# Two weight sums per gate/up quad from a DRAM scratch, and a fourth quad per chunk, in a one-core decoder layer

## Chip, cores, metric

The kernel runs on one core of a Trainium2 chip. The metric is the device time of one execution in microseconds. The kernel before took 1198.18 us, the median of three runs (1197.95 to 1198.29).

## What is computed

One decoder layer on 256 tokens of width 2048: a head stage (eight attention heads and a gated short convolution) with its output projection, a cross-attention over 256 memory tokens, and a SwiGLU feed-forward of width 5632, each behind an RMS norm, then a last norm. All in float32. The change is in the feed-forward:

```python
def swiglu(h, w_gate, w_up, w_down):
    return (jax.nn.silu(h @ w_gate) * (h @ w_up)) @ w_down

h = rms_norm(x, g_ffn[l])
x = x + swiglu(h, w_gate[l], w_up[l], w_down[l])
```

## The kernel before

**Tiles and steps.** The weights lie in DRAM as one stream (`w_stream`) of tiles of 128 x 1024 floats, 512 KB each: two blocks of 128 rows (k) by 512 columns. SP loads them in order into the four slots of `raw`. Each tile passes three stations. ACT casts it to `whi` (`chunk_cast`, its line L1145; L893 ahead of the feed-forward). DVE subtracts and leaves the rest in `wlo` (the split, L1624; L1270 earlier). PE multiplies: a product of one token tile (128 tokens) with one block is three matmuls of 512 columns, hi x hi, hi x lo and lo x hi (L489 to L491, in quads L732 to L734). A direct step uses a whole tile for both token tiles, which makes 12 matmuls. `whi` and `wlo` have four slots too.

**What orders the work.** Each engine has a hand-written order, and semaphores count the steps: `w_loaded` (landed), `hi_ready` (cast), `lo_ready` (split done), `step_used` (PE done). The cast of step v waits until PE has used step v - 4 (`step_used` at v - RING + 1). SP loads into a slot of `raw` when the split of what lay there is done. Instructions of an engine go in order, so a waiting one holds those behind it.

**Chunks and quads.** Gate and up (each 2048 x 5632) are computed in 11 chunks of 512 columns (`NFC`). In a chunk, eight pairs of k blocks (2 x 128 rows) meet two token tiles and two matrices. A pair takes either two direct steps (24 matmuls), or a quad: Winograd's form of Strassen's product with 7 products in place of 8 (21 matmuls). A quad needs sums of the activations (`s_forms`, made once, ahead of chunk 0: forms `sfh`, `sfl` and a part of `ahi`, `alo`) and sums of the weights b11, b12, b21, b22, made anew in every quad. It stands in the order of steps as four parts. Before, three of the eight pairs are quads, at steps 3, 9 and 14 of a chunk of 22 steps (`QUADS`, `QUAD_AT`, `CHUNK`), and DVE makes the weight sums beside its splits: two of 512 columns in `raw` (L1619, L1627) and one of 1024 columns in `wsum` (L1631).

**Around the quads.** At step 2 of a chunk PE transposes the last chunk's result in two units (L521; ACT and DVE split it at step 3, DVE's line L1279). After the last quad DVE combines the products (`combine`), ACT applies silu (`gate`), and at step 0 of the next chunk DVE finishes the chunk (`up`, L1585 and L1588).

**GpSimd (POOL)** computes the rotary products of the heads (`rope`, L441 to L445), the inverse roots of the heads (`head_root`, L449) and norms (`root`), and a part of the convolution. It issues no transfer. Ahead of the feed-forward SP's loads are a plain loop of four per turn (L382 to L385), in it a loop of 16 per chunk (L386 to L393), where three wait for weight sums in place of splits:

```python
with sp.Fori(0, NFC) as ci:
    for n in range(CHUNK_RAW):
        done = RAW_DONE[n - RING]
        if done is None:
            sp.wait_ge(w_sums, ci * (3 * QUADS) + SUMMED[n - RING])
        else:
            sp.wait_ge(lo_ready, ci * CHUNK + (J_FF + done - (CHUNK if n < RING else 0)))
```

## Time and profile before

| | |
|---|---|
| median of three runs | 1198.18 us |
| the profiled execution, its own time | 1197.7 us |
| its span, first to last instruction | 1196.0 us |
| PE busy | 1184.9 us, 99% |
| DVE busy | 930.3 us, 78% |
| ACT busy | 673.6 us, 56% |
| POOL busy | 83.6 us, 7% |
| DMA | 234.52 MB, 196 GB/s over the span |

The span is compared with the execution's own time, which is 1.7 us longer. The rows on which the prediction rests stand below, by view. In a timeline a row has the start (us from the span's beginning), the duration, engine, line, operation, operands, and in brackets how long the engine was idle before it and what released it. A matmul of 512 columns is shown with 0.39 us, but the next one starts before it has ended.

### The profile page before, as it was taken

The numbers are of one execution on the slowest core, as the hardware profiler recorded it, in microseconds if no ns is written. First come the engines' busy times: TensorE is split into PE (matmuls) and PEld (weight loads), VectorE is DVE, ScalarE is ACT, GpSimd is POOL, SyncE is SP. The second block draws the span as 40 slices with busy tenths as digits, with TensorE's granted clock in tenths as the row PEclk, the third lists the DMA queues.
The fourth block names the chain that finished last, engine by engine and source line by source line (L and its number), as shares of the span: only waits on it lengthen the run. The fifth ranks groups of instructions, "written<-read, shape, count | busy, mean of one in ns | idle before, by whom it ended". The sixth has DMA issues, their size and how long they took to land.

```text
span 1196.0 us, 16405 instructions
## 1 busy us (share of the span) xinstructions
PE 1184.9 (99%) x5421; PEld 982.6 (82%) x5421; DVE 930.3 (78%) x1171; ACT 673.6 (56%) x881; POOL 83.6 (7%) x89
## 2 busy tenths in 40 slices
PE   9999999999999999999999999999999999999997
PEld 7888888888888888888888888888888888888885
DVE  5755555557855666999899899989989889978886
ACT  5665555445744575756556555655555554545553
POOL 0042332200210000000000000000000000000000
PEclk9999999999999999999999999999999999999999
DMA  9865455556556544466666566566655666665663
GB/s 340 296 211 173 162 175 177 174 176 222 166 187 185 191 158 141 159 212 186 202 197 205 176 210 225 166 202 198 209 187 199 213 211 203 211 216 174 200 206 141
DMA packets 65851, 234.52 MB, mean 196 GB/s; under 512 B 7696, under 2 KB 8464, under 8 KB 65424
## 3 DMA queue, kind: packets, MB, share of 16 engines
q1 hardware_dynamic: 63072, 225.60, 57.6%
q10 hardware_dynamic: 2736, 8.35, 1.8%
q8 instruction: 26, 0.43, 0.2%
q14 instruction: 17, 0.14, 0.0%
HBM read 231.83 MB, written 2.10 MB: 196 GB/s over the span
## 4 chain that ended last, share of the span: by engine, by line
PE 93%; DVE 4%; DMA 1%; ACT 1%; issue 1%; SPq 0%; POOLq 0%; POOL 0%; ACTq 0%; DVEq 0%
PE ps L489 24%; PE ps L491 24%; PE ps L490 24%; PE ps L732 6%; PE ps L734 6%; PE ps L733 6%; DVE wlo L1624 2%; PE ps L521 1%; DMA raw<-w_stream 1%; DVE alo L1282 0%; PE ps L604 0%; DVE wlo L1270 0%; PE ps L559 0%; PE ps L564 0%; PE ps L688 0%
## 5 line engine op out<-in xcount | busy, mean ns | idle before, releaser
L1145 ACT ACTIVATE whi<-raw 128x1024 fp32r<-128x1024 f32 (+1 forms) x309 | 303.5, 992 | 216.6 <-PE ps L491 91.5
L1624 DVE TENSOR_TENSOR wlo<-raw,whi 128x1024 fp32r<-128x1024 f32 (+1 forms) x309 | 345.5, 1137 | 25.1 <-ACT whi L1145 24.3
L1270 DVE TENSOR_TENSOR wlo<-raw,whi 128x1024 fp32r<-128x1024 f32 x160 | 198.4, 1245 | 110.9 <-ACT whi L893 110.7
L489 PE MATMUL ps<-whi,ahi 128*128 128x512 f32 x600 | 235.6, 393 | 0.0
L491 PE MATMUL ps<-whi,alo 128*128 128x512 f32 x600 | 233.7, 390 | 0.0
L490 PE MATMUL ps<-wlo,ahi 128*128 128x512 f32 x600 | 233.5, 389 | 0.0
L893 ACT ACTIVATE whi<-raw 128x1024 fp32r<-128x1024 f32 x160 | 168.4, 1058 | 106.9 <-PE ps L491 94.0
L489 PE MATMUL ps<-whi,bhi 128*128 128x512 f32 x448 | 180.0, 402 | 1.5 <-DVE blo L1363 1.0
L491 PE MATMUL ps<-whi,blo 128*128 128x512 f32 x448 | 175.1, 391 | 0.0
L490 PE MATMUL ps<-wlo,bhi 128*128 128x512 f32 x448 | 174.5, 389 | 0.0
L491 PEld LDWEIGHTS ps<-whi,alo 128*128 128x128 f32 x600 | 112.6, 188 | 23.7
L490 PEld LDWEIGHTS ps<-wlo,ahi 128*128 128x128 f32 x600 | 112.7, 188 | 22.8
L489 PEld LDWEIGHTS ps<-whi,ahi 128*128 128x128 f32 x600 | 112.7, 188 | 22.6
L491 PEld LDWEIGHTS ps<-whi,blo 128*128 128x128 f32 x448 | 84.1, 188 | 18.3
L489 PEld LDWEIGHTS ps<-whi,bhi 128*128 128x128 f32 x448 | 84.2, 188 | 18.1 <-DVE blo L1363 1.2
L490 PEld LDWEIGHTS ps<-wlo,bhi 128*128 128x128 f32 x448 | 84.3, 188 | 16.4
L489 PE MATMUL ps<-whi,fhi 128*128 128x512 f32 x240 | 93.7, 390 | 0.2 <-DVE wlo L1624 0.2
L491 PE MATMUL ps<-whi,flo 128*128 128x512 f32 x240 | 93.4, 389 | 0.0
L490 PE MATMUL ps<-wlo,fhi 128*128 128x512 f32 x240 | 93.4, 389 | 0.0
L1145 ACT ACTIVATE whi<-wsum 128x1024 fp32r<-128x1024 f32 x47 | 49.9, 1062 | 68.8 <-PE ps L491 50.7
L1624 DVE TENSOR_TENSOR wlo<-wsum,whi 128x1024 fp32r<-128x1024 f32 x47 | 57.6, 1225 | 35.7 <-ACT whi L1145 34.9
L1631 DVE TENSOR_TENSOR wsum<-raw 128x1024 f32<-128x1024 f32 x47 | 57.2, 1217 | 0.0
(244 smaller groups left out, 1488.1 us busy)
## 6 DMA issues: line engine op xcount, KB each, us to landing
raw<-w_stream SPq DMA_DIRECT2D x422, 512.0 KB, 4.1
res<-x_in ACTq DMA_DIRECT2D x4, 512.0 KB, 7.9
stage<-mem_in ACTq DMA_DIRECT2D x4, 512.0 KB, 6.1
proj<-mem_T ACTq DMA_DIRECT2D x2, 1024.0 KB, 7.8
stage<-x_T SPq DMA_DIRECT2D x7, 256.0 KB, 7.5
y_out<-res SPq DMA_DIRECT2D x4, 320.0 KB, 3.0
raw<-w_stream SPq DMA_DIRECT2D x4, 256.0 KB, 4.8
gfin<-g_final ACTq DMA_DIRECT2D x1, 1024.0 KB, 4.8
```

The lines of the kernel that those rows point to most:

```text
L489: nc.tensor.matmul(bank, lhsT=a_h, rhs=w_h, start=start, stop=False)
L490: nc.tensor.matmul(bank, lhsT=a_h, rhs=w_l, start=False, stop=False)
L491: return nc.tensor.matmul(bank, lhsT=a_l, rhs=w_h, start=False, stop=stop)
L521: done = nc.tensor.transpose(bank[:, n, t * P:(t + 1) * P], src[:, t, (k + n) * P:(k + n + 1) * P], ident[:])
L732: nc.tensor.matmul(ps[:, bank, :], lhsT=a[0], rhs=w[0], start=start, stop=False)
L733: nc.tensor.matmul(ps[:, bank, :], lhsT=a[0], rhs=w[1], start=False, stop=False)
L734: return nc.tensor.matmul(ps[:, bank, :], lhsT=a[1], rhs=w[0], start=False, stop=stop)
L893: nc.scalar.activation(tile_pair(whi, j), tile_pair(raw, j), ACT.Copy).then_inc(hi_ready, 1)
L1145: nc.scalar.activation(whi_here, src, ACT.Copy).then_inc(hi_ready, 1)
L1270: vec.tensor_tensor(tile_pair(wlo, j), tile_pair(raw, j), tile_pair(whi, j).bitcast(f32), ALU.subtract).then_inc(lo_ready, 1)
L1624: vec.tensor_tensor(lo_here, src, hi_here.bitcast(f32), ALU.subtract).then_inc(lo_ready, 1)
L1631: vec.tensor_tensor(wsum[:].rearrange("p (h n) -> p h n", h=2), both, b22.unsqueeze(1).to_broadcast([P, 2, GC]), ALU.subtract).then_inc(w_ ...
```

## The change

The weights of the quads are laid out anew. For every quad the stream has a tile z = [b11 | b22] and a tile w = [b21 | b12]. A new DRAM tensor `tsums` has 44 tiles of 512 KB, one per quad of each chunk.

- **Copies.** SP copies z into `tsums`, DRAM to DRAM, 44 in all: one behind every fourth load from load 19 on (36 of them), and one at the end of each of the first 8 chunks.
- **Adds.** POOL adds b12 to both halves of the copy with an accumulating transfer (`add_weights`; two reads of b12, 256 pieces of 2 KB), in order; each waits for its copy and for the landing of the add before it. One stands behind the first two ropes, two behind every `rope` in the heads' loop, 16 beside the convolution and the output projection (one per three steps of `j`), four between `root(2)` and `root(3)`, the last 11 in a loop behind that.
- **Loads.** Per quad SP loads z (512 KB), the b21 half of w (256 KB), and the summed tile into the new single buffer `t13` (512 KB, shown as t_110 in the built order). The next `t13` load waits until the split of the last one (part 2) is done.
- **Quads.** Four pairs are quads, at steps 2, 7, 12 and 17 of a chunk of 24 steps, with one direct step between them. Part 0 uses z (6 matmuls), part 1 the half tile b21 (3 matmuls), part 2 `t13` (6), part 3 `wsum` (6). DVE makes two sums of 512 columns, `wsum` = [t13 left + b22 | that + b21], once `t13` is cast.
- The forms of the activations are now of four pairs, in other places of the memory, with changed signs. `p1_copy`, `combine` and `gate` stand at steps 19, 21 and 23 (before: 17, 18 and 21).

The diff, cut to its core:

```diff
-QUADS = 3
+QUADS = 4
-QUAD_AT = (3, 9, 14)
+QUAD_AT = (2, 7, 12, 17)
-GATE_STEPS = {0: 3, 1: 4, 2: 5, 7: 6, 8: 7}
-UP_STEPS = {13: 3, 18: 4, 19: 5, 20: 6, 21: 7}
+GATE_STEPS = {0: 4, 1: 5, 6: 6, 11: 7}
+UP_STEPS = {16: 4, 21: 5, 22: 6, 23: 7}
+RAW_TILES = ("D0", "D1", "Z0", "H0", "D2", "Z1", "H1", "D3", "Z2", "H2", "D4", "Z3", "H3", "D5", "D6", "D7")
+SUMMED = {2: 1, 3: 2, 5: 3, 6: 4, 8: 5, 9: 6, 11: 7}
+T_LOAD_AT = {1: 0, 8: 1, 11: 2, 14: 3}
-UNITS_AT, P1_AT, COMBINED, SILU_AT = 2, 17, 18, 21
+UNITS_AT, P1_AT, COMBINED, SILU_AT = 2, 19, 21, 23
...
+            def load_chunk(ci):
+                for n, name in enumerate(RAW_TILES):
+                    kind, q = name[0], int(name[1:])
+                    if n in T_LOAD_AT:
+                        m = T_LOAD_AT[n]
+                        if m == 0:
+                            sp.wait_ge(t_summed, ci * (16 * QUADS) + 16 * QUADS)
+                        else:
+                            sp.wait_ge(lo_ready, ci * CHUNK + (J_FF + QUAD_AT[m - 1] + 3))
+                        sp.dma_start(t13[:], tsums[ci * QUADS + m]).then_inc(t_loaded, 16)
+                    last = (n - RING) % CHUNK_RAW
+                    if last in SUMMED:
+                        sp.wait_ge(w_sums, ci * (2 * QUADS) + SUMMED[last])
...
+            with sp.Fori(COPY_FROM + 1, J_FF // RING) as i:
+                load_four(i)
+                sp.wait_ge(t_copied, i * 16 + (-16 * COPY_FROM))
+                sp.dma_start(tsums[i - COPY_FROM], stream[i + (J_Z - COPY_FROM)]).then_inc(t_copied, 16)
+            with sp.Fori(0, LATE_COPIES) as ci:
+                load_chunk(ci)
+                sp.wait_ge(t_copied, ci * 16 + 16 * (TSUMS - LATE_COPIES))
+                sp.dma_start(tsums[ci + (TSUMS - LATE_COPIES)],
+                             stream[ci + (J_Z + TSUMS - LATE_COPIES)]).then_inc(t_copied, 16)
...
+            def add_weights(m, first=False):
+                pool.wait_ge(t_copied, m * 16 + 16)
+                if not first:
+                    pool.wait_ge(t_summed, m * 16)
+                both = tsums[m].rearrange("p (h n) -> p h n", h=2)
+                b12 = stream[m + J_W][:, GC:KS * GC].unsqueeze(1).to_broadcast([P, 2, GC])
+                nc.gpsimd.dma_start(both, b12, accum_op=ALU.add).then_inc(t_summed, 16)
...
                     rope(h + 2, n)
+                    for m in range(2):
+                        add_weights(i * 4 + (2 * n + m + 1))
...
                 if part == 0:
+                    product(4, a_block(0, 0), left, opens, closes)
                     done = product(up_banks[0], s_form(3), right, opens, False)
                 if part == 1:
-                    done = product(gate_banks[0], a_block(0, 1), right, False, closes)
+                    done = product(gate_banks[0], a_block(0, 1), left, False, closes)
+                if part == 2:
+                    p5 = product(5, s_form(0), left, opens, closes)
...
                     if opens:
                         pe.wait_ge(unit_lo, ci * 2 + (U_FF + 2 * c - 1))
-                    product(6, s_form(2), left, opens, closes)
+                    done = product(6, s_form(2), right, opens, closes)
+                if part == 3:
+                    product(7, s_form(1), left, opens, closes)
                     done = product(gate_banks[1], a_block(1, 1), right, False, closes)
...
+                if part == 2:
+                    act.wait_ge(t_loaded, ci * (16 * QUADS) + 16 * (q + 1))
+                    src = t13[:]
+                if part == 3:
+                    act.wait_ge(w_sums, ci * (2 * QUADS) + 2 * (q + 1))
+                    src = wsum[:]
+                act.wait_ge(step_used, ci * CHUNK + (v - RING + 1))
+                nc.scalar.activation(whi_here, src, ACT.Copy).then_inc(hi_ready, 1)
...
+                dve.wait_ge(hi_ready, ci * CHUNK + (v + 1))
...
+                if part == 2:
+                    b22, b21 = tile_pair(raw, j)[:, GC:KS * GC], tile_pair(raw, j + 1)[:, 0:GC]
+                    vec.tensor_tensor(wsum[:, 0:GC], t13[:, 0:GC], b22, ALU.add).then_inc(w_sums, 1)
+                    dve.wait_ge(w_sums, ci * (2 * QUADS) + (2 * q + 1))
+                    vec.tensor_tensor(wsum[:, GC:KS * GC], wsum[:, 0:GC], b21, ALU.add).then_inc(w_sums, 1)
+                    src = t13[:]
+                if part == 3:
+                    src = wsum[:]
+                vec.tensor_tensor(lo_here, src, hi_here.bitcast(f32), ALU.subtract).then_inc(lo_ready, 1)
```

DVE in a chunk, one quad and the direct step behind it, in the order before:

```order
L1619 TENSOR_TENSOR raw<-raw 128x512 [waits hi_ready]
L1624 TENSOR_TENSOR wlo<-raw,whi 128x512
L1626 REGISTER_ALU
L1627 TENSOR_TENSOR raw<-raw 128x512 [waits w_sums]
L1616 REGISTER_ALU
L1624 TENSOR_TENSOR wlo<-raw,whi 128x1024 [waits hi_ready]
L1629 REGISTER_ALU
L1631 TENSOR_TENSOR wsum<-raw 128x1024 [waits w_sums]
L1616 REGISTER_ALU
L1624 TENSOR_TENSOR wlo<-raw,whi 128x1024 [waits hi_ready]
L1616 REGISTER_ALU
L1624 TENSOR_TENSOR wlo<-wsum,whi 128x1024 [waits hi_ready]
```

and now (L1736 and L1738 are the two sums, L1742 a split):

```order
L1742 TENSOR_TENSOR wlo<-raw,whi 128x1024 [waits hi_ready]
L1731 REGISTER_ALU
L1742 TENSOR_TENSOR wlo<-raw,whi 128x512 [waits hi_ready]
L1731 REGISTER_ALU
L1736 TENSOR_TENSOR wsum<-t_110,raw 128x512 [waits hi_ready]
L1737 REGISTER_ALU
L1738 TENSOR_TENSOR wsum<-wsum,raw 128x512 [waits w_sums]
L1742 TENSOR_TENSOR wlo<-t_110,whi 128x1024
L1731 REGISTER_ALU
L1742 TENSOR_TENSOR wlo<-wsum,whi 128x1024 [waits hi_ready]
```

Three sums in different parts have become two in part 2, ahead of the split of `t13` and behind its cast.

SP in a chunk, from the load that waits for the first quad's weights on, before:

```order
L390 ISA
L393 ISA [waits w_sums]
L393 DMA raw<-w_stream 128x1024
L392 REGISTER_ALU
L393 ISA [waits lo_ready]
L393 DMA raw<-w_stream 128x1024
L392 REGISTER_ALU
L393 ISA [waits lo_ready]
L393 DMA raw<-w_stream 128x1024
L392 REGISTER_ALU
L393 ISA [waits lo_ready]
L393 DMA raw<-w_stream 128x1024
```

and now, from the half tile of the second quad on:

```order
L421 REGISTER_ALU
L429 ISA [waits w_sums]
L429 DMA raw<-w_stream 128x512
L421 REGISTER_ALU
L425 ISA [waits w_sums]
L425 DMA raw<-w_stream 128x1024
L417 REGISTER_ALU
L418 ISA [waits lo_ready]
L418 DMA t_110<-tsums 128x1024
L423 REGISTER_ALU
L427 ISA [waits lo_ready]
L427 DMA raw<-w_stream 128x1024
```

The load of `t13` waits for `lo_ready` and stands directly behind a half tile and a whole tile, which wait for the two sums.

POOL in the heads' loop, where one `head_root` followed the last addition of `rope` (L445), now:

```order
L497 TENSOR_TENSOR qkr<-rtmp 128x4x64 [waits rope_products]
L498 TENSOR_TENSOR qkr<-rtmp 128x4x64
L506 ISA
L511 ISA [waits t_summed,t_copied]
L511 DMA tsums<-w_stream 256x1x512
L506 ISA
L511 ISA [waits t_summed,t_copied]
L511 DMA tsums<-w_stream 256x1x512
L502 TENSOR_TENSOR small<-small,mhalf 128x2 [waits o_var]
```

Two waits for the copies and the adds, and two transfers, stand ahead of the next head's root (L502).

## Rows read from the trace of the kernel before

**Rows 1.** The page: busy time, share of the span and instructions by engine.
```profile
PE 1184.9 (99%) x5421; PEld 982.6 (82%) x5421; DVE 930.3 (78%) x1171; ACT 673.6 (56%) x881; POOL 83.6 (7%) x89
```

**Rows 2.** Windows: us, busy per engine, clock, DMA share and GB/s, two stages.
```profile
240.00:490.00 250.00, 249.93 (x1201) 208.58 (x1200) 166.04 (x254) 141.47 (x232) 17.69 (x19) 1.00 0.54 177
...
490.00:950.00 460.00, 459.61 (x2071) 380.67 (x2069) 419.65 (x473) 267.85 (x300) 1.59 (x1) 1.00 0.61 197
```

**Rows 3.** The page: chain that ended last, shares by engine.
```profile
PE 93%; DVE 4%; DMA 1%; ACT 1%; issue 1%; SPq 0%; POOLq 0%; POOL 0%; ACTq 0%; DVEq 0%
```

**Rows 4.** Timeline of PE in one chunk: start, us, line, operands, count.
```profile
574.85 0.39 PE L489 MATMUL ps<-whi,ahi 128*128 128x512 f32 x1
...
580.30 1.03 PE L521 MATMUL ps<-ident,fact 128*128 128x128 f32 x8
```

**Rows 5.** Windows: the same columns, one chunk, transposes to transposes.
```profile
580.30:622.67 42.37, 42.37 (x192) 35.19 (x191) 38.42 (x45) 24.25 (x27) 0.00 (x0) 1.00 0.61 199
```

**Rows 6.** Timeline of DVE in the same chunk.
```profile
574.57 0.68 DVE L1585 TENSOR_TENSOR fact<-ps,fact 128x512 f32<-128x512 f32 x1
...
575.29 0.75 DVE L1588 SCALAR_TENSOR_TENSOR fact<-fact,rstd,silu 128x512 f32<-128x512 f32 x1
...
577.34 0.68 DVE L1619 TENSOR_TENSOR raw<-raw 128x512 f32<-128x512 f32 x1
...
585.20 1.23 DVE L1624 TENSOR_TENSOR wlo<-wsum,whi 128x1024 fp32r<-128x1024 f32 x1 [1.18 <-ACT whi L1145]
...
586.34 2.35 DVE L1624 TENSOR_TENSOR wlo<-raw,whi 128x1024 fp32r<-128x1024 f32 x2
```

**Rows 7.** Timeline of ACT, then of the SP queue, in that chunk.
```profile
584.11 1.06 ACT L1145 ACTIVATE whi<-wsum 128x1024 fp32r<-128x1024 f32 x1 [1.57 <-PE ps L491]
...
607.48 1.06 ACT L1145 ACTIVATE whi<-raw 128x1024 fp32r<-128x1024 f32 x1 [1.12 <-DMA raw<-w_stream]
...
588.87 0.33 SPq L393 DMA_DIRECT2D raw<-w_stream  x1
...
603.14 0.33 SPq L393 DMA_DIRECT2D raw<-w_stream  x1
```

**Rows 8.** DMA issues from 601.9, 603, 594 and 605.5 us: count, KB, us to landing.
```profile
raw<-w_stream SPq DMA_DIRECT2D x1, 512.0 KB, 3.2
...
raw<-w_stream SPq DMA_DIRECT2D x1, 512.0 KB, 4.2
...
raw<-w_stream SPq DMA_DIRECT2D x1, 512.0 KB, 4.4
...
raw<-w_stream SPq DMA_DIRECT2D x3, 512.0 KB, 4.7
```

**Rows 9.** Timelines of PE and DVE where chunk 0 begins.
```profile
489.00 0.39 PE L489 MATMUL ps<-whi,ahi 128*128 128x512 f32 x1
...
501.99 0.50 PE L732 MATMUL ps<-whi,sfh 128*128 128x512 f32 x1 [0.38 <-DVE wlo L1624]
...
485.17 0.55 DVE L1549 TENSOR_TENSOR asum<-araw 128x384 f32<-128x384 f32 x1
...
488.31 1.65 DVE L1282 SCALAR_TENSOR_TENSOR alo<-ps,par,ahi 128x256 fp32r<-128x256 f32 x4
...
492.67 1.35 DVE L1561 TENSOR_TENSOR sfl<-asum,sfh 128x1152 fp32r<-128x1152 f32 x1
...
499.15 1.65 DVE L1282 SCALAR_TENSOR_TENSOR alo<-ps,par,ahi 128x256 fp32r<-128x256 f32 x4
```

**Rows 10.** DMA from 85 to 490 us: queue, packets, MB, share; then the issues.
```profile
q1 hardware_dynamic: 18894, 68.80, 51.9%
...
raw<-w_stream SPq DMA_DIRECT2D x131, 512.0 KB, 3.3
```

**Rows 11.** Waits: who waited for whom, us in total, times, longest us.
```profile
ACT whi L893 <- PE ps L491: 94.0, 73, 1.9
...
POOL small L449 <- DVE small L1412: 134.4, 8, 23.6
```

More of the change, by code:

```diff
@@ L261, in build @@
         fat = [shared]
+        late_tiles = FF // P - 2 * KS
+        s3_at = [fat[0] + 4 * late_tiles * SEQ]
+        s3h = sb("s3h", [P, 3, P], f32r, at=s3_at)
+        s3l = sb("s3l", [P, 3, P], f32r, at=s3_at)
         fhi = sb("fhi", [P, FF // P, SEQ], f32r, at=fat)
+        assert s3_at[0] <= fat[0]
+        t13_at = [fat[0] + 4 * late_tiles * SEQ]
+        t13 = sb("t13", [P, KS * GC], at=t13_at)
         flo = sb("flo", [P, FF // P, SEQ], f32r, at=fat)
+        assert t13_at[0] <= fat[0]
         silu = sb("silu", [P, TT, GC], at=fat)
@@ new lines, in _ @@
+            with sp.Fori(3, COPY_FROM) as i:
+                load_four(i)
+            load_four(COPY_FROM)
+            sp.dma_start(tsums[0], stream[J_Z]).then_inc(t_copied, 16)
+            with sp.Fori(COPY_FROM + 1, J_FF // RING) as i:
+                load_four(i)
+                sp.wait_ge(t_copied, i * 16 + (-16 * COPY_FROM))
[5 more added lines that the diff above has]
+                             stream[ci + (J_Z + TSUMS - LATE_COPIES)]).then_inc(t_copied, 16)
@@ L394, in _ @@
+            with sp.Fori(LATE_COPIES, NFC) as ci:
+                load_chunk(ci)
             for j in range(RING):
@@ L457, in _ @@
             rope(1, 1)
+            add_weights(0, first=True)
             with pool.Fori(0, NH // 2 - 1) as i:
@@ L474, in _ @@
                                             ALU.subtract).then_inc(merged_conv, 1)
+                if j % 3 == 0:
+                    add_weights(m)
+                    m += 1
             root(2)
+            for m in range(m, m + 4):
+                add_weights(m)
             root(3)
+            with pool.Fori(m + 1, TSUMS) as i:
+                add_weights(i)
             for t in range(TT):
@@ L750, in s_form @@
                         return [b[:, KS * n, P:2 * P] for b in (ahi, alo)]
+                    if n == QUADS - 1:
+                        return [b[:, f - 1, :] for b in (s3h, s3l)]
                     return [b[:, f - 1, n, :] for b in (sfh, sfl)]
@@ L1149, in chunk_cast @@
                 v, j, q, part = chunk_place(c, p)
-                sums = 0 if part is None else ci * (3 * QUADS) + 3 * q
-                part_cast(v, j, part, sums, ci * CHUNK, ci * CHUNK_RAW)
+                if part is None:
+                    part_cast(v, j, None, 0, ci * CHUNK, ci * CHUNK_RAW)
+                    return
+                whi_here, src = whi[:, v % RING, :], tile_pair(raw, j)
+                if part == 0:
+                    act.wait_ge(w_loaded[j % RING], loaded_by(j, ci * CHUNK_RAW))
+                if part == 1:
+                    act.wait_ge(w_loaded[(j + 1) % RING], loaded_by(j + 1, ci * CHUNK_RAW))
+                    whi_here, src = whi_here[:, 0:GC], tile_pair(raw, j + 1)[:, 0:GC]
+                if part == 2:
[6 more added lines that the diff above has]
+                nc.scalar.activation(whi_here, src, ACT.Copy).then_inc(hi_ready, 1)
             def down_cast(i):
@@ L1636, in chunk_split @@
                 v, j, q, part = chunk_place(c, p)
-                if part == 1 and q == 0:
-                    dve.wait_ge(s_lo, 1)
-                part_split(v, j, part, 0 if part is None else ci * (3 * QUADS) + 3 * q, ci * CHUNK)
+                if part is None:
+                    part_split(v, j, None, 0, ci * CHUNK)
+                    return
+                hi_here, lo_here, src = whi[:, v % RING, :], wlo[:, v % RING, :], tile_pair(raw, j)
+                dve.wait_ge(hi_ready, ci * CHUNK + (v + 1))
+                if part == 1:
+                    hi_here, lo_here, src = hi_here[:, 0:GC], lo_here[:, 0:GC], tile_pair(raw, j + 1)[:, 0:GC]
+                if part == 2:
[7 more added lines that the diff above has]
+                vec.tensor_tensor(lo_here, src, hi_here.bitcast(f32), ALU.subtract).then_inc(lo_ready, 1)
             def down_split(i):
```

87 lines of the change are left out of this document (47 added, 40 removed).

## The prediction

> **What bounds the kernel now.** I read the page first: PE is busy in 1184.9 of 1196.0 us [rows 1], and the chain that ended last is 93% PE [rows 3]. The windows by stage show PE full ahead of the feed-forward and inside it, at full clock [rows 2]. Then one chunk: PE has no gap in its 42.37 us, DVE is busy in 38.42, ACT in 24.25 [rows 5]. From the chunk's first matmul to the transposes at step 2 are 24 matmuls in 5.45 us, 0.227 us each [rows 4]; 183 of them make 41.49 us, so the eight transposes cost 0.88. Whatever PE need not do is a gain, as long as casts, splits and loads keep up. DVE, 91% busy, and the loads are what to watch.
>
> **What PE saves.** A pair as a quad has 21 matmuls in place of 24: 3 x 0.227 = 0.68 us per chunk, 7.5 us in 11 chunks. The chunk falls to 41.69.
>
> **DVE and ACT by amount.** A split of 1024 columns costs 1.14 us (two in 2.35, less the overlap at the end [rows 6]), an operation of 512 columns 0.61. Before, a quad had 4 x 1.14 + 3 x 0.61 = 6.4 us on DVE, now 3 x 1.14 + 3 x 0.61 = 5.25. So a chunk goes from 10 x 1.14 + 3 x 6.4 to 8 x 1.14 + 4 x 5.25, 30.6 to 30.1: nothing. ACT gets 1.5 casts more of 1.06 us [rows 7] and has 18 us idle: nothing. The amount is hidden by PE's 41.7 us; the order is not.
>
> **The new chain.** `t13` is one buffer. The next summed tile is loaded only when the split of the last one is done; the cast waits for the landing; both sums wait for the cast; the split stands behind the sums. From one such split's end to the next:
> - SP's issue, 0.18: two splits end at 586.34 + 2.35 = 588.69, the load goes out at 588.87 [rows 6, 7];
> - the load, L;
> - landing to cast, 0.14: issued at 603.14, 4.2 us on its way, cast at 607.48 [rows 7, 8];
> - the cast 1.06, and 0.03 to DVE: 584.11 to 585.20 [rows 6, 7];
> - the first sum to the second, which needs it, 0.72 (574.57 to 575.29 [rows 6]), the second 0.61, the split 1.23.
>
> That is L + 3.97. PE asks for a new one after a quad and a direct step, 33 x 0.227 = 7.48 us.
>
> **L.** A load with nothing before it lands in 3.2 us, one issued about 1.1 us behind another in 4.2 to 4.4, three in a row have a median of 4.7 [rows 8]. The `t13` load goes out 1.15 us behind a whole tile (issued at the second sum) and 1.9 behind a half tile (at the first). The nearest rows are the second of a pair, 4.4, and three in a row, 4.7; the third tile in front is only half as large, so I take 4.45. The link is 8.42 us, 0.94 more than PE's 7.48.
>
> **What that costs a chunk.** Times from the start of step 0. PE reaches part 2 of the four quads at 8.36, 15.84, 23.32 and 30.80 (two steps 5.45, transposes 0.88, then 9 matmuls into each quad). First split: behind the last chunk's fourth `t13` split DVE has seven splits, `combine` (six of 0.61) and `up` (2.77, 574.57 to 577.34 [rows 6]), 14.4 us, against 10.9 of PE's; so `up` ends near 3.5, then the half tile's split and the sums: 6.7. It is in time. The second load goes out at 6.88 and lands at 11.33, just as PE frees the slot of `whi` (11.08); split done at 15.1, in time by 0.7. Third: 23.5, late by 0.2. Fourth: 31.95, late by 1.15 in all. Two stops also slow the first matmul behind them, 0.50 for 0.39 as at 501.99 [rows 9], 0.2 together. A chunk takes 41.69 + 1.15 + 0.2 = 43.05 against 42.37: +0.68, ten chunks **+6.8 us**. The slack of the order is the only cover, and each 0.1 us of L more costs 0.3 per chunk.
>
> **Chunk 0.** It now begins with pair 4, whose `alo` comes in the batch at 488.31. Four forms of 512 columns in place of four of 384 (0.55 each [rows 9]) delay that by 0.5; the first half is done at 489.7, and PE starts chunk 0 at 489.00 [rows 9]: 0.7 late. The first quad comes one direct step earlier, and product 6 waits for the low part of unit 6, which DVE makes behind the split of part 3: the batch at 499.15 [rows 9] comes no earlier, its first half near 500.2, PE wants it at 499.1: with part 2 itself 1.5 late in all. The 0.38 wait at 501.99 goes. With three more refills and the later links, 0.9, chunk 0 costs 0.7 + 1.5 + 0.9 + 0.3 - 0.4 - 0.68 = **+2.3** (0 to 4).
>
> **Copies and adds ahead of the feed-forward.** A load of 512 KB takes 51.9% x 405 / 131 = 1.6 us of the 16 DMA engines [rows 10]. Four loads (12.4 us of time) now have one copy and one add beside them. No row shows DRAM to DRAM; a copy moves the bytes once in and once out, so one to two loads' worth; an add reads two tiles' worth and writes one, one to three. Low, 6 x 1.6 = 9.6 us of 12.4: hidden. High, 9 x 1.6 = 14.4: 2 us more per four loads, 36 times, 72 us. I take the low-to-middle case, zero: these loads land in 3.3 us [rows 10], and from issue to the cast that PE allows are four steps less cast and split, 4 x 2.72 - 2.4 = 8.5 us; most casts wait for PE, 94.0 us in 73 waits [rows 11]. The cover is gone if copy plus add cost over 3.7 loads' worth. The Trainium skill, DMA: Bandwidth & Descriptors, "Latency and other measured facts", gives copies between HBM tensors 207 to 214 GB/s, which would make the copy 2.5 us; no run here shows it.
>
> SP's own wait for the copy before is 12 us old when it comes: nothing. POOL waits, ahead of a head's root, for the first of two adds to land. It sits idle 134.4 us before eight roots [rows 11], 16.8 per head; an add below that delays nobody. `root(2)` and `root(3)` have adds before them whose copies were issued many steps earlier: nothing. The 8 late copies and last 11 adds fall behind the last quad, where PE has five direct steps: nothing, up to 1.3 us per chunk if they push a `t13` load.
>
> **Sum.** 6.8 + 2.3 + 0 = +9.1 on the profiled execution's 1197.7 us: 1206.8. The median of the runs is 0.5 above that execution, so I forecast **1207 us**, its own range 1201 (L = 4.3) to 1217 (L = 4.7: the chunk +1.4, with chunk 0 about +17).
>
> **Rival 1, the tile is in time: faster.** If L is 4.0 or less, the second split ends at 14.9 and the fourth at 14.9 + 2 x 7.97 = 30.8, just when PE asks. Then every chunk but the first saves 0.68, chunk 0 costs some 1.5: -6.8 + 1.5, **1193 us**; without chunk 0's loss 1191. For it: half a tile is in front, not a whole one, and a lone load has 3.2. Against it: no load of the rows that had another 1.1 us before it landed under 4.2. It decides at L = 4.0. The Trainium skill's fit in the same page ("Anatomy of one DMA") is 2.0 us plus the bytes at 436 GB/s, 3.2 us for this tile, and speaks for this rival; the trace agrees for a lone load only.
>
> **Rival 2, it cancels.** L of 4.15 to 4.3: the fourth split is 0.2 to 0.7 late, and a chunk neither gains nor loses more than 0.3 us. **1198 us.**
>
> **Rival 3, the DMA engines fill up ahead of the feed-forward: much slower.** Copy plus add cost 4.5 loads' worth: 8.5 x 1.6 = 13.6 per 12.4 us, 1.2 x 36 = 43 us, on top of the forecast **1250**. Casts then wait for loads in the heads' stage, and POOL's adds reach its roots. Against it: a DMA share of 0.54 there [rows 2], and a share of time in which packets are under way is not all service. The order shows all copies, adds and quads in place, so that the change is not made is no case.
>
> **Chances.** Forecast 0.45, rival 1 0.30, rival 2 0.17, rival 3 0.08. A measurement tells this kernel from no change at about 0.2% (2.4 us). Faster 0.30, same 0.17, slower 0.53. The range that holds it 8 times in 10 reaches from rival 1's best, 1191, to L = 4.7, 1217; since cases of both signs count, the forecast's own range is the one above.
>
> **What would show it.** Matmuls fall by 33; PE's busy time of quads and steps falls by 7.5. Right: in a chunk the loads `t_110<-tsums` take 4.3 to 4.7 us, ACT's cast of `t13` is idle behind that DMA, and PE waits for DVE's split L1742 in the third and fourth quad, about 1.2 us per chunk of 43 us. Windows from the heads to 490 us keep their length and matmuls. Wrong in the chain: `t13` lands in under 4.1 us, the chunk takes 41.7. Wrong ahead of it: chunk 0 starts after 492 us, ACT's casts wait for `raw<-w_stream`, or POOL's root L502 comes late. Also wrong: PE waits for `raw` tiles and not for `t13`.

## The result and the profile after

The changed kernel takes **1242.37 us** (median of four runs, 1239.4 to 1243.1) against 1198.24 us of the kernel before on the same chip: a ratio of 1.0364, with a 95% interval of 1.0351 to 1.0377. It is slower, as forecast, but by 44 us where 9 were expected, and it lies outside the range. The profiled execution took 1243.1 us.

The page of the changed kernel: engines (answering [rows 1]), two of the queues, and the shares of the chain that ended last (answering [rows 3]):

```profile
PE 1194.0 (96%) x5388; PEld 974.7 (79%) x5388; DVE 937.2 (76%) x1183; ACT 685.2 (55%) x906; POOL 127.4 (10%) x133
...
q1 hardware_dynamic: 70816, 260.21, 60.8%
q0 software_dynamic: 11968, 23.07, 11.9%
...
PE 47%; DMA 21%; DVE 14%; issue 11%; ACT 6%; SPq 1%; DVEq 0%; ACTq 0%; POOL 0%; POOLq 0%
PE ps L562 13%; PE ps L564 13%; PE ps L563 13%; DMA t<-tsums 11%; DMA raw<-w_stream 8%; ACT whi L1241 4%; DVE wlo L1742 4%; DVE wlo L1714 3%; DVE wsum L1736 2%; PE ps L805 1%; PE ps L807 1%; PE ps L806 1%; DVE fact L1675 1%; DMA tsums<-w_stream 1%; DVE wsum L1738 1%
```

33 matmuls are gone, as planned. But the chain, 93% PE before, is now 47% PE, 21% DMA and 14% DVE: PE no longer sets the end by itself. Where it lost is in the windows of the changed kernel: from the heads to the feed-forward (two stretches), the feed-forward, then a chunk beside copies and adds, and one behind the last of them (answering [rows 2, 5]):

```profile
66.00:240.00 174.00, 174.00 (x821) 144.37 (x820) 98.71 (x143) 92.55 (x143) 72.69 (x68) 1.00 0.86 259
240.00:490.00 250.00, 249.04 (x1195) 207.36 (x1194) 166.13 (x249) 139.78 (x231) 37.21 (x39) 1.00 0.88 262
490.00:950.00 460.00, 424.81 (x1851) 337.76 (x1850) 384.78 (x440) 255.44 (x296) 12.38 (x12) 1.00 0.70 222
...
596.90:643.80 46.90, 44.20 (x189) 35.74 (x190) 38.97 (x45) 25.43 (x29) 1.03 (x1) 0.96 0.69 224
...
963.00:1006.70 43.70, 42.66 (x189) 34.38 (x188) 39.17 (x45) 24.62 (x28) 0.00 (x0) 1.00 0.64 214
```

Ahead of the feed-forward PE has no gap to speak of, though the DMA share went from 0.54 to 0.88. The transposes of `res` that stood at 485.36 us before stand at 486.92: 1.6 us. In the feed-forward PE is idle for 35 us. I follow it by the transposes of `fact`, one set per chunk. Before, the first stands at 537.8 us and chunks take 42.4. Now the first stands at 547.8, and the ten periods behind it are 49.1, 46.9, 45.8, 47.9, 45.5, 45.1, 45.2, 45.1, 44.8 and 43.7. So **10 us are lost up to and in chunk 0, and 35 in the ten chunks behind it**; what follows is as long as before (234.5 us to the end against 234.2).

The waits of the changed kernel (who waited for whom, us in total, times, longest; answering [rows 11]):

```profile
POOL tsums L511 <- DMA tsums<-w_stream: 494.0, 32, 46.7
...
ACT whi L1241 <- DVE wsum L1738: 84.4, 41, 4.6
ACT whi L1220 <- DMA raw<-w_stream: 77.9, 37, 4.4
POOL small L502 <- DVE small L1502: 74.0, 8, 23.6
ACT whi L1241 <- DMA t<-tsums: 64.4, 32, 3.1
```

ACT waits for DMA in casts of `t13` and of `raw` tiles. The sum of the waits for `raw` doesn't tell the loss: the kernel before has 86.1 us of them in 60 waits. POOL's eight roots (L502) still wait for DVE: the adds never reached them. What PE waits for, from 545 to 1010 us, is always DVE, and before it had no such wait there:

```profile
PE ps L805 <- DVE wlo L1742: 14.3, 21, 1.3
PE ps L594 <- DVE fact L1678: 8.8, 6, 2.3
PE ps L805 <- DVE flo L1369: 7.1, 8, 0.9
```

The first row is the wait of the forecast, for the split of `t13`. The second is for `up`, ahead of the transposes, and the third for the unit's low part; for the chunks behind chunk 0 the forecast had neither.

### The profile page after: what moved, and what is told of

It reads as the page before. It is cut to its first block, busy times and chain, and to the rows that moved or that the text cites. A ratio compares the mean times of both kernels' runs of the same rounds, so it can differ in the third digit from the quotient of the medians.

```text
span 1241.2 us, 17006 instructions
## 1 busy us (share of the span) xinstructions
PE 1194.0 (96%) x5388; PEld 974.7 (79%) x5388; DVE 937.2 (76%) x1183; ACT 685.2 (55%) x906; POOL 127.4 (10%) x133
## 4 chain that ended last, share of the span: by engine, by line
PE 47%; DMA 21%; DVE 14%; issue 11%; ACT 6%; SPq 1%; DVEq 0%; ACTq 0%; POOL 0%; POOLq 0%
PE ps L562 13%; PE ps L564 13%; PE ps L563 13%; DMA t<-tsums 11%; DMA raw<-w_stream 8%; ACT whi L1241 4%; DVE wlo L1742 4%; DVE wlo L1714 3%; DVE wsum L1736 2%; PE ps L805 1%; PE ps L807 1%; PE ps L806 1%; DVE fact L1675 1%; DMA tsums<-w_stream 1%; DVE wsum L1738 1%
## 5 line engine op out<-in xcount | busy, mean ns | idle before, releaser
L1360 DVE TENSOR_TENSOR wlo<-raw,whi 128x1024 fp32r<-128x1024 f32 x160 | 200.4, 1256 | 115.4 <-ACT whi L968 115.1
L1220 ACT ACTIVATE whi<-raw 128x1024 fp32r<-128x1024 f32 (+1 forms) x188 | 189.5, 1022 | 128.8 <-DMA raw<-w_stream 77.9
L1714 DVE TENSOR_TENSOR wlo<-raw,whi 128x1024 fp32r<-128x1024 f32 (+1 forms) x188 | 219.3, 1181 | 29.2 <-ACT whi L1220 28.8
L562 PE MATMUL ps<-whi,ahi 128*128 128x512 f32 x512 | 200.9, 392 | 4.7 <-DVE wlo L1714 3.3
L564 PE MATMUL ps<-whi,alo 128*128 128x512 f32 x512 | 199.4, 390 | 0.0
L563 PE MATMUL ps<-wlo,ahi 128*128 128x512 f32 x512 | 199.2, 389 | 0.0
L562 PEld LDWEIGHTS ps<-whi,ahi 128*128 128x128 f32 x512 | 96.1, 188 | 25.9 <-issue 3.2
L564 PEld LDWEIGHTS ps<-whi,alo 128*128 128x128 f32 x512 | 96.1, 188 | 20.2
L563 PEld LDWEIGHTS ps<-wlo,ahi 128*128 128x128 f32 x512 | 96.2, 188 | 19.6
L511 POOL DMA_DIRECT2D tsums<-w_stream x44 | 46.2, 1051 | 494.0 <-DMA tsums<-w_stream 494.0
L1742 DVE TENSOR_TENSOR wlo<-raw,whi 128x1024 fp32r<-128x1024 f32 x88 | 81.2, 953 | 12.5 <-ACT whi L1241 12.5
```

The costliest lines, as they stand in the source:

```text
L511: nc.gpsimd.dma_start(both, b12, accum_op=ALU.add).then_inc(t_summed, 16)
L562: nc.tensor.matmul(bank, lhsT=a_h, rhs=w_h, start=start, stop=False)
L563: nc.tensor.matmul(bank, lhsT=a_h, rhs=w_l, start=False, stop=False)
L564: return nc.tensor.matmul(bank, lhsT=a_l, rhs=w_h, start=False, stop=stop)
L1220: nc.scalar.activation(whi_here, src, ACT.Copy).then_inc(hi_ready, 1)
L1360: vec.tensor_tensor(tile_pair(wlo, j), tile_pair(raw, j), tile_pair(whi, j).bitcast(f32), ALU.subtract).then_inc(lo_ready, 1)
```

## The experiments

Twelve kernels ran, in comparison with the kernel before (1198.0 to 1198.2 us in each group). My theory after the first trace: the t13 chain costs more than forecast, and late copies and adds, costed at nothing, cost the rest.

### 1. Without the scratch, and with the sums ahead of the cast

`e1_no_scratch`: all copies and adds out, their waits too, and

```diff
-                        sp.dma_start(t13[:], tsums[ci * QUADS + m]).then_inc(t_loaded, 16)
+                        sp.dma_start(t13[:], stream[ci * QUADS + (J_Z + m)]).then_inc(t_loaded, 16)
```

> Leaves out the copies and the adds; t13 is loaded from z in the stream, so b12 is missing in two sums of each quad. Theory A (copies and adds beside the feed-forward delay the loads where one chunk turns into the next; the t13 chain costs only what was forecast): every chunk takes the 43.7 us that the last one took in the changed kernel, chunk 0 some 3 us more than before, in all 1211 to 1218 us. Theory B (the t13 chain itself costs the 45 us per chunk, the transfers nothing): chunks stay at 45 us and more, 1230 us and over.

Measured: 1221.17 us, 1.0191 [1.0174, 1.0208], between the two theories. Chunks take 44.3 in the mean. The scratch is 21 us of the 44, and 23 remain without it.

`e2_early_sums`, the full computation:

```diff
+                if part == 2:
+                    dve.wait_ge(lo_ready, ci * CHUNK + (v - 2))
+                    dve.wait_ge(t_loaded, ci * (16 * QUADS) + 16 * (q + 1))
+                else:
+                    dve.wait_ge(hi_ready, ci * CHUNK + (v + 1))
...
                     src = t13[:]
+                    dve.wait_ge(hi_ready, ci * CHUNK + (v + 1))
```

> Computes everything. DVE makes the two sums as soon as t13 has landed, beside ACT's cast, and not behind it: a link of the chain is 1.33 us shorter (L + 2.6). Theory A: the stops in the third and fourth quad go, those at the turn of the chunk stay; a chunk beside a copy and an add gains about 1.3 us of 45.1, in all 1225 to 1233 us. Theory B: the chain falls below PE's 7.48 us per quad and nearly all is gained, 1192 to 1200 us.

Measured: 1215.45 us, 1.0139 [1.0122, 1.0156], 27 less than the change. That gain is more than theory A allows and far less than theory B's. The link is not 1.33 us shorter, as I had written, but 1.09: the two sums take 1.33, the cast and the step to DVE that they now stand beside take 1.09.

`e3_both` is the two edits together.

> Both edits: no copies, no adds (b12 is missing in two sums of each quad), sums beside the cast. Both theories: chunks at PE's own 41.7 to 42.0 us; only chunk 0 is later than before, 1191 to 1197 us. If it stays over 1200, a third cause slows the chunks, in the order of the steps itself.

Measured: 1197.86 us, 0.9995 [0.9985, 1.0004], 0.9 over the range, with chunks of 42.2 in the mean. Making the sums while ACT casts takes 23.3 us off e1, and it is enough to undo all that the chain had cost. With the scratch and early sums (e2) the time is 17.6 us over e3: the scratch costs nearly as much where the chain is cured as where it is not (21.2).

### 2. The scratch, taken apart

`e4_no_late` keeps 36 copies and 33 adds ahead of the feed-forward, and leaves the 8 late copies and 11 adds out; `t13` is loaded from `tsums[ci * 2 + m]`. `e5_late_copies` has the 8 copies back. `e6_late_adds` has 11 adds back, on tiles that nobody loads.

```diff
-            with pool.Fori(m + 1, TSUMS) as i:
-                add_weights(i)
+            for i in range(3):
+                other_add(i)
+            with pool.Fori(0, LATE_COPIES) as ci:
+                pool.wait_ge(lo_ready, ci * CHUNK + (J_FF + 22))
+                other_add(ci + 3)
```

> Keeps the 36 copies and 33 adds ahead of the feed-forward, leaves out the 8 copies and 11 adds beside it; t13 is loaded from the first 24 tiles of the scratch, so most quads have the wrong weight sums. Theory A: within 3 us of the kernel without any scratch traffic (the stage ahead has room). Rival C (the copies and adds ahead of the feed-forward cost time too, or reading back from the scratch is slower than from the stream): more than 5 us slower than that kernel.

> The kernel without late copies and adds (e4_no_late, 1226.5 us), with the 8 copies at the ends of the first 8 chunks put back and no add beside the feed-forward; t13 from the first 24 scratch tiles, so most weight sums are wrong. Theory C (the copy, in the same queue ahead of the next chunk's first load and t13, delays them): most of the 16 us between e4_no_late and the changed kernel comes back, 1236 to 1242 us. Theory D (the adds, which share the 16 DMA engines, do it): 1226 to 1231 us.

> The kernel without late copies and adds, with 11 adds put back and no copies: three at once when the feed-forward begins, then one per chunk behind its last quad, on tiles that no load reads (most weight sums are wrong). Theory C: 1226 to 1231 us. Theory D: 1236 to 1242 us, and loads under way beside an add take 6 us and more. If both this and the copies alone cost 3 us or less, only the two together fill the DMA engines.

Measured: e4 1226.48 us (1.0242 [1.0225, 1.0259]), e5 1236.20 (1.0315 [1.0299, 1.0331]), e6 1232.59 (1.0296 [1.0280, 1.0311]). Late copies cost 9.7 us, late adds 6.1, and the change is 15.9 above e4: the two add up, each difference being good to about 3 us. So theories C and D hold both, each in part (e5 is in C's range, e6 between the two ranges), and e4, 5.3 over e1, falls to rival C by a little. **Of the scratch's 21 us, 16 are the 19 late transfers.** The other 5.3 I then asked for with `e11_read_stream`, which is e4 with `t13` from the stream:

```diff
-                        sp.dma_start(t13[:], tsums[ci * 2 + m]).then_inc(t_loaded, 16)
+                        sp.dma_start(t13[:], stream[ci * QUADS + (J_Z + m)]).then_inc(t_loaded, 16)
```

> As e4 (36 copies and 33 adds ahead of the feed-forward, none beside it), but t13 is loaded from the weight stream (tile z), so that the product is not the layer's and the scratch is written and never read. It tells apart where e4's 5.3 us over e1 come from. If from the traffic ahead of chunk 0: as e4, 1226. If from reading the scratch back: as e1, 1221.

Measured: 1224.34 us, 1.0226 [1.0209, 1.0243]. It lies between e1 and e4, 3.2 above the one and 2.1 below the other, each with an interval of 2 us on either side. Of these the 3.2 is just clear of the noise of a difference (about 2.9 us), the 2.1 is not. So part of it is probably the traffic ahead, and what the rest is stays open. The traces don't show where: the second transposes of `res` stand at 479.93 us in e1, 481.07 in e11 and 479.54 in e4, which has the same traffic ahead as e11. Nor does a load from the scratch land later: 4.6 us in the median in e4, 4.7 from the stream in e11.

### 3. The product that asks for the unit's low part

The order of e3 let PE wait in part 2 for DVE's split of the last chunk's unit. `e7_swap` is e3 with products exchanged, so that part 3 asks for it:

```diff
+                    done = product(7, s_form(2), right, opens, closes)
+                if part == 3:
                     if opens:
                         pe.wait_ge(unit_lo, ci * 2 + (U_FF + 2 * c - 1))
-                    done = product(6, s_form(2), right, opens, closes)
-                if part == 3:
-                    product(7, s_form(1), left, opens, closes)
+                    product(6, s_form(1), left, opens, closes)
```

> The kernel with no scratch and the early sums (e3_both, 1197.9 us; b12 missing in two sums of each quad), and the third product of part 2 goes to the bank that no unit uses, so PE's wait for the low part of the last chunk's unit moves from part 2 to part 3. Theory E (what is left over PE's own 41.7 us in a chunk, and 1.2 us of chunk 0, is this wait): chunks of 41.7 to 41.8, in all 1190 to 1194 us. Rival F (loads or splits hold PE there anyway): 1196 to 1199 us.

Measured: 1195.81 us, 0.9982 [0.9973, 0.9991], between theory and rival; the chunks are theory E's. One of them in the windows of this kernel:

```profile
582.70:624.40 41.70, 41.70 (x190) 34.63 (x189) 38.34 (x44) 25.52 (x29) 0.00 (x0) 1.00 0.68 227
```

41.7 us without a gap on PE is what PE needs for four quads. So all that four quads give in this order, with summed tiles that cost nothing, is 2.2 us. In the traces its ten chunks take 418.4 us against 424.0, and of these 5.6 us the stretch up to chunk 0's end loses 2.1 (first transposes of `fact` at 539.9 against 537.8) and the one behind the last chunk 1.9 (236.1 against 234.2; why was not looked into).

### 4. The scratch with everything cured

`e8_all_ahead` is the full computation: early sums, exchanged products, all 44 copies ahead (in every fourth turn one more), 39 adds ahead, and five adds left beside chunk 0:

```diff
+                        if s == RING - 1 or (k == 1 and s == 1):
+                            sp.wait_ge(t_copied, g * 80 + 16 * made)
+                            sp.dma_start(tsums[g * 5 + made], stream[g * 5 + (J_Z + made)]).then_inc(t_copied, 16)
+                            made += 1
```

> Computes everything: early sums, the bank swap, and all 44 copies ahead of the feed-forward (an extra one in every fourth turn), with 6 more adds ahead of it; 5 adds are left in chunks 0 and 1. If the late transfers cost 16 us and the stage ahead has room: 1191 to 1198 us, at or under the kernel before. Rival (the stage ahead is full at 1.2 copies and an add per four loads): chunk 0 begins more than 3 us later than in the changed kernel, 1200 us and over.

Measured: 1203.80 us, 1.0044 [1.0030, 1.0057], the best of the full kernels, 38.6 under the change and 5.8 above before. The time is the rival's, but not for its reason: the second transposes of `res` come 0.9 us later than in the changed kernel (481.46 against 480.56), not over 3. Its chunks behind chunk 0 are near e7's. It loses 3.1 us ahead of the feed-forward (transposes of `res` at 481.46 against e7's 478.38), and 5.0 from there through chunk 0. The windows of e8 for that stretch and one chunk:

```profile
487.80:548.00 60.20, 54.42 (x233) 42.70 (x232) 51.77 (x67) 37.28 (x46) 6.21 (x6) 0.97 0.79 223
590.80:633.20 42.40, 42.33 (x190) 34.40 (x189) 39.14 (x45) 25.32 (x29) 0.00 (x0) 1.00 0.67 223
```

and of e7 for the same stretch, 5.0 us shorter:

```profile
484.70:539.90 55.20, 52.25 (x234) 41.61 (x232) 49.69 (x64) 37.05 (x46) 1.06 (x1) 1.00 0.57 191
```

Can those five adds be had for less if they are spread? `e9_paced5` sends them one per chunk in chunks 1 to 5, `e10_paced9` nine of them in chunks 0 to 8 (four ahead between the roots in place of eight):

```diff
-            with pool.Fori(m + 1, TSUMS) as i:
-                add_weights(i)
+            with pool.Fori(0, 5) as i:
+                pool.wait_ge(lo_ready, i * CHUNK + (J_FF + 1 * CHUNK + 17))
+                add_weights(i + 39)
```

> As e8 (all copies ahead, early sums, swapped products, full computation), but the last five adds go out one per chunk, in chunks 1 to 5, behind step 17, in place of back to back beside chunk 0. Theory (adds beside the loads of chunk 0 delay its tiles and let PE stand long enough for its clock to halve): chunk 0 falls from e8's by the gaps that e7 does not have, about 5 us, the paced adds cost up to 0.3 us each, 1199 to 1201. Rival (chunk 0 is late because of the adds still under way from the stage ahead, which stay): 1203 to 1204.

> As e9, but nine adds are left for the feed-forward, one per chunk behind step 17 of chunks 0 to 8, and only four stand between root(2) and root(3). Theory that traffic just ahead of chunk 0 holds its loads back: chunk 0 begins up to 3 us earlier than in e8 (481.46 us for its first transposes' counterpart, e7 478.38) and the time is 1197 to 1199, level with before. Theory that each add beside the feed-forward costs what the late adds cost in e6 less e4 (6.1 us for 11, 0.55 each): 9 x 0.55 = 5 on e7's 1195.8, 1201 or more.

Measured: e9 1207.18 us (1.0091 [1.0073, 1.0108]), e10 1215.37 (1.0142 [1.0127, 1.0157]). The theories missed, but for the "1201 or more" of e10, which had 0.55 us per add behind it. e9's six runs reach from 1204.97 to 1212.90, and its trace is of the fastest. In e9 the stretch of chunk 0 fell to 54.6 us, as expected, but the five chunks with an add rose by 1.0 to 2.1 us each over e7's, 7.3 in all, where 0.3 each was expected. In e10 the eight periods with an add are 17.5 us longer than e7's, **2.2 us per add**. Its transposes of `res` stand at 481.09, 0.4 us before e8's, where up to 3 were expected: four adds less between the roots did next to nothing, so the 3 us are lost earlier or to other traffic; which, no run shows.

The DMA issues of e10 around one add, issued at 609.87 us (count, KB each, median us from issue to landing): first the load issued at 612.33, then the one at 616.73.

```profile
raw<-w_stream SPq DMA_DIRECT2D x1, 512.0 KB, 7.1
...
raw<-w_stream SPq DMA_DIRECT2D x1, 512.0 KB, 6.7
```

and what this does to ACT and PE, in their timelines of e10:

```profile
619.57 1.06 ACT L1231 ACTIVATE whi<-raw 128x1024 fp32r<-128x1024 f32 x1 [2.96 <-DMA raw<-w_stream]
...
623.52 1.06 ACT L1231 ACTIVATE whi<-raw 128x1024 fp32r<-128x1024 f32 x1 [1.61 <-DMA raw<-w_stream]
...
626.79 0.50 PE L573 MATMUL ps<-whi,ahi 128*128 128x512 f32 x1 [1.16 <-DVE wlo L1725]
```

In e7, without an add, the two loads in these places (issued at 604.91 and 610.06) land in 4.1 and 6.0 us. Issued 2.5 us behind an add the first takes 7.1; ACT's cast waits 2.96 us for it, where in e7 it doesn't wait. The waits of ACT alone don't tell the loss, since in e7 the last cast of the three waits 3.02 us for its load and PE doesn't stop. In e10 PE stops for 1.16 us, by the starts of its matmuls 1.4 of the 2.2 us that this chunk lost. In e6 an add cost 0.55 us (6.1 / 11), in e10 2.2. There the chunks differ (44 us and 41.7 us), and the place too (behind step 22 and behind step 17); which of the two makes the difference was not tried.

### 5. What the chain is: a loop

e1's chunk is 44.3 where the forecast had 43.05. The trace of e1 shows the chain link by link. From its DVE timeline, the split of `t13` in the fourth quad of one chunk, then the wait behind `combine`, the first `t13` split of the next chunk, and those that follow:

```profile
748.44 1.22 DVE L1724 TENSOR_TENSOR wlo<-t,whi 128x1024 fp32r<-128x1024 f32 x1
...
761.27 1.23 DVE L1724 TENSOR_TENSOR wlo<-raw,whi 128x1024 fp32r<-128x1024 f32 x1 [0.81 <-ACT whi L1223]
...
764.52 0.75 DVE L1660 SCALAR_TENSOR_TENSOR fact<-fact,rstd,silu 128x512 f32<-128x512 f32 x1
...
767.12 1.22 DVE L1724 TENSOR_TENSOR wlo<-t,whi 128x1024 fp32r<-128x1024 f32 x1
...
775.52 1.22 DVE L1724 TENSOR_TENSOR wlo<-t,whi 128x1024 fp32r<-128x1024 f32 x1
...
782.74 0.69 DVE L1718 TENSOR_TENSOR wsum<-t,raw 128x512 f32<-128x512 f32 x1 [1.83 <-ACT whi L1223]
...
784.07 1.22 DVE L1724 TENSOR_TENSOR wlo<-t,whi 128x1024 fp32r<-128x1024 f32 x1
...
792.46 1.22 DVE L1724 TENSOR_TENSOR wlo<-t,whi 128x1024 fp32r<-128x1024 f32 x1
```

and from its SP and ACT timelines, one link in between:

```profile
776.76 0.33 SPq L416 DMA_DIRECT2D t<-w_stream  x1
...
781.64 1.06 ACT L1223 ACTIVATE whi<-t 128x1024 fp32r<-128x1024 f32 x1 [2.22 <-DMA t<-w_stream]
```

The splits of the chunk start at 767.12, 775.52, 784.07 and 792.46: links of 8.40, 8.55 and 8.39, where I had forecast 8.42. The way round, from the fourth split to the first of the next chunk, is 767.12 - 748.44 = 18.68. Together 44.02, the period of this chunk (44.0). That the starts add up is no finding; that nothing in the circle waits for PE is: in all three links the cast waited for the landing (1.16, 2.22 and 2.28 us in ACT's timeline), and on the way round DVE waits once, 0.81 us for ACT. (ACT's cast of the first `t13` does wait for PE, but ends at 764.73, before DVE comes to the sums.) So in this chunk a loop of one buffer sets the time, with PE running behind it: by the starts of its matmuls PE loses 0.56 us at the unit's low part, 0.74 in the third quad and 0.85 in the fourth, 2.2 of the 2.3 us between 41.7 and 44.0. To test it, `e12_two_buffers` gives `t13` a second buffer, puts its loads one quad earlier in SP's order, and leaves the sums behind the cast:

```diff
-T_LOAD_AT = {1: 0, 8: 1, 11: 2, 14: 3}
+T_LOAD_AT = {1: 0, 5: 1, 8: 2, 11: 3}
...
-                        if m:
-                            sp.wait_ge(lo_ready, ci * CHUNK + (J_FF + QUAD_AT[m - 1] + 3))
-                        sp.dma_start(t13[:], stream[ci * QUADS + (J_Z + m)]).then_inc(t_loaded, 16)
+                        if m > 1:
+                            sp.wait_ge(lo_ready, ci * CHUNK + (J_FF + QUAD_AT[m - 2] + 3))
+                        sp.dma_start((res[:, 0, 0:KS * GC] if m % 2 else t13[:]), stream[ci * QUADS + (J_Z + m)]).then_inc(t_loaded, 16)
```

> As e1 (no copies, no adds, t13 filled from the weight stream, sums behind ACT's cast), but the tiles of the second and fourth quad go to a part of the residual's memory, so that t13 has two buffers and a load waits for the split of the quad before last; the loads stand one quad earlier in SP's order. The residual is lost, so that the output is not the layer's. Theory (e1's chunk is a loop of one buffer: 18.72 us from the fourth split of t13 to the next first one, then three links of 8.4 to 8.55, 44.1 in all): the loop is cut, the chunk is 41.7 plus up to 0.5 for the wait for the unit's low part, 41.9 to 42.2, and the time 1196 to 1199. Rival (what costs e1 is that both sums stand behind the cast, as e2 and e3 took exactly that away): the chunk stays at 44, and the time at 1219 to 1221.

Measured: 1198.28 us, 1.0003 [0.9993, 1.0013], chunks of 41.7 to 42.0 behind the first of 43.1. The windows of e12 for a stretch as long as a chunk:

```profile
721.80:763.90 42.10, 42.10 (x191) 34.87 (x191) 39.30 (x45) 26.03 (x31) 0.00 (x0) 1.00 0.67 226
```

This confirms the loop: it is what cost 23 us. Early sums (e3) shorten each link by the cast, which brings it from 8.4 to 7.2 to 7.8 us in most links of e3's trace, about PE's 7.48; a second buffer takes the load out of the link; either is enough. e12 takes its second buffer (4 KB per partition) from the residual and so is a test and no improvement; e3's way needs no memory.

## Why the prediction was right and wrong

**Right.** PE's saving: a chunk without other losses is 41.7 us (e7), as forecast. (183 x 0.227 is 41.54, not 41.49; nothing rests on it.) The link: 8.39 to 8.55 for 8.42, but in part by luck. The `t13` loads take 4.6, 4.8 and 4.6 us in e1's chunk, 4.7 in the median, the upper of my two bounds and not the 4.45 of the sum; SP issues them 0.02 to 0.03 us behind the split in place of 0.18. The two errors nearly cancel. Copies and adds ahead of the feed-forward: nearly hidden, 5.3 us at most (e4). The DMA issues of the changed kernel from 66 to 490 us (answering [rows 10]):

```profile
q1 hardware_dynamic: 21203, 90.84, 58.9%
q0 software_dynamic: 8976, 17.30, 26.8%
...
raw<-w_stream SPq DMA_DIRECT2D x137, 512.0 KB, 5.7
tsums<-w_stream SPq DMA_DIRECT2D x34, 512.0 KB, 6.1
tsums<-w_stream POOLq DMA_DIRECT2D x33, 512.0 KB, 8.7
```

An add costs 26.8% x 424 / 33 = 3.4 us of the 16 engines, 2.1 loads' worth; loads and copies together (58.9% x 424 / 171) 1.5 each, so a copy is about one. Four loads with a copy and an add are 7.1 x 1.6 = 11.4 us of 12.4, in the middle of my case and hidden. Loads land in 5.7 us where 3.3 were seen [rows 10], below the 8.5 that the order allows. Rival 3 is out, and so is rival 2, which needed an L of 4.15 to 4.3.

**Wrong, and the largest part of a miss of 35 us: "The 8 late copies and last 11 adds fall behind the last quad, where PE has five direct steps: nothing, up to 1.3 us per chunk".** They cost 15.9 us, and the "up to 1.3" stood neither in the sum nor in the range. In the traces of the changed kernel and e4 they cost 4.6 us up to the first transposes of `fact` (three adds go out beside chunk 0) and 14.0 in the ten chunks behind it: 4.4 in the first, 1.4 to 3.4 in the next four, 0.5 to 0.8 in four more, and none in the last. I counted PE's direct steps, where nothing waits for `t13`, as cover. But SP runs some 10 us ahead: beside PE's last direct steps it loads the next chunk's tiles, the first `t13` and z among them. The SP queue of the changed kernel at one turn (PE reaches the transposes at step 2 at 873.2):

```profile
855.56 0.57 SPq L443 DMA_DIRECT2D tsums<-w_stream  x1
858.02 0.34 SPq L425 DMA_DIRECT2D raw<-w_stream  x1
858.65 0.33 SPq L418 DMA_DIRECT2D t<-tsums  x1
859.25 0.33 SPq L425 DMA_DIRECT2D raw<-w_stream  x1
860.37 0.33 SPq L427 DMA_DIRECT2D raw<-w_stream  x1
861.51 0.33 SPq L429 DMA_DIRECT2D raw<-w_stream  x1
```

The landings of these, by the DMA issues of windows of 0.1 us: the copy 4.9, then 4.5, 5.8 (`t13`), 6.5, 7.5, and the half tile at 861.51 8.5 us; the add that the copy set off went out at 861.17 and took 9.2. ACT in the same window:

```profile
862.66 1.06 ACT L1220 ACTIVATE whi<-raw 128x1024 fp32r<-128x1024 f32 x1 [2.77 <-DMA raw<-w_stream]
865.83 1.06 ACT L1220 ACTIVATE whi<-raw 128x1024 fp32r<-128x1024 f32 x1 [2.12 <-DMA raw<-w_stream]
```

In e1's turn at 751 us, without copy and add, the same five loads land in 3.4, 4.2, 5.6, 5.8 and 5.1 us: they crowd each other there as well, but each lands 0.9 to 3.4 us sooner. The two casts ahead of the cast of z wait 4.9 us, in e1 3.9 (1.58 and 2.33 in its ACT timeline), and the half tile's cast 1.04 more (at 870.11), in e1 nothing. Of these 2 us half reaches the way round. The fourth `t13` split and the next chunk's first, in DVE's timeline of the changed kernel:

```profile
855.30 1.22 DVE L1742 TENSOR_TENSOR wlo<-t,whi 128x1024 fp32r<-128x1024 f32 x1
...
874.95 1.22 DVE L1742 TENSOR_TENSOR wlo<-t,whi 128x1024 fp32r<-128x1024 f32 x1
```

The way round is 19.65 us here and 18.68 in e1. Over the ten loops from chunk 0's first `t13` split on, the changed kernel takes 19.9 us more than e1, 17.0 of them on the ways round (24.2, 22.0, 21.0, 20.4, 21.8, 20.3, 19.3, 19.7, 19.0 and, behind the last copy and add, 18.4) and 2.9 in the links. So the late transfers act on the turn of the chunk, as the forecast did not have it. The loop is not a condition for it: e2 less e3, 17.6 us, is nearly as much with the links cured, and e10's adds cost 2.2 us each in chunks that PE bounds.

**Wrong in size: "A chunk takes 41.69 + 1.15 + 0.2 = 43.05".** The links came out right, but the way round was worked out as 14.4 us from the fourth split to the end of `up`. It is (764.52 + 0.75) - (748.44 + 1.22) = 15.6: DVE stands 0.81 us behind ACT's cast of z, which is behind `gate` (silu) and a cast that waits for its load, and the operations themselves take 0.4 more. So the "in time by 0.7" of the second split was no slack: every 0.1 us on the way round makes the chunk 0.1 longer. By my own numbers the loop was 14.4 + 3.2 + 3 x 8.42 = 42.9, and laid over PE's times it had come to 41.69 + 1.15 = 42.8, the same. Summing the circle would not have found the miss; its mis-sized term is the way round, 1.2 us too short, and that is all of the 1.2 between 42.8 and 44.0. A wait that I did not list for any chunk but the first, PE in part 2 of the first quad for the unit's low part, costs 0.3 us per chunk where PE sets the time (e3 less e7). In e1 it can't be added to the loop, since PE waits there for DVE anyway. Together e1's ten chunks are 443.2 us against 424.0 of before, +19.2 where I had 6.8; the first four of them are 0.4 to 1.3 us longer than the later ones, which I have not explained.

**Wrong in size: chunk 0, "+2.3 (0 to 4)".** Up to the first `fact` transposes e7 loses 2.1 us, e1 5.2, the change 10. That 2.1 is near 2.3 confirms no term of it: e7 has no late links and has moved product 6, two terms of 0.9 and up to 1.5 us, and e3, which leaves product 6 where it was, loses 1.8. The late chain (e1 less e7) costs 3.1 where the sum had 0.9 for it, and 4.8 more come with the scratch. By e4, only 0.2 over e1 at this point, nearly all of that is the late transfers again.

The runs in a row, each less its neighbour: exchanged products and early sums without scratch (e7) -2.2, the unit's wait (e3) +2.1, the loop (e1) +23.3, traffic ahead and reading it back (e4) +5.3, the late transfers +15.9: 44.4. They add up to the measured 44.1 by their making, but for the 0.2 us between the medians of the kernel before; what they show is the share of each.

**Rival 1** had put its point of decision at L = 4.0; the medians of the `t13` loads in the runs are 4.5 to 4.7. The fit of the Trainium skill, DMA: Bandwidth & Descriptors, "Anatomy of one DMA", that I weighed there is given for one transfer that GpSimd issues, and as an estimate makes 3.2 us for the tile. For SP's loads beside others e1's trace has 4.7 in the median. The trace decides, and it was early sums and exchanged products together (e7), at L = 4.6, that reached rival 1's chunk of 41.7.

## What to carry to other kernels

A single buffer that is loaded, cast, summed, split and loaded again is a closed loop: add up its links and the way round over a whole period, the waits on the way round too, and compare that sum with the engine that you think is the bound. Take a short operation out of the link (sums beside the cast) or give it a second buffer; here each was worth 23 us. And extra transfers are nearly hidden where loads have slack against the engine that waits last, 8.5 us here ahead of the feed-forward. Ask beside which loads they will run, and not which matmuls run at that time; beside a feed-forward that asks for each tile soon after it lands, a 512 KB add cost 0.6 to 2.2 us, bundled or spread.
